# Eight late tiles of a Hyena convolution: their three-tap convolutions and gates go from VectorE to GpSimd

## The reference, cut to what matters

```python
def short_conv(u, w, b):
    L = u.shape[1]
    pad = HY_SHORT // 2
    up = jnp.pad(u, ((0, 0), (pad, pad), (0, 0)))
    return sum(up[:, j:j + L] * w[j] for j in range(HY_SHORT)) + b
...
    p = h @ w_in
    u = short_conv(p[..., :(HY_ORDER + 1) * HY_WIDTH], conv_w, conv_b)
    gate = p[..., (HY_ORDER + 1) * HY_WIDTH:]
    parts = jnp.split(u, HY_ORDER + 1, axis=-1)
    k_f = hyena_filters(L, f_w1, f_b1, f_w2, f_b2, f_w3, f_b3, freq)
    z = parts[0]
    for o in range(HY_ORDER):
        z = parts[o + 1] * long_conv(z, k_f[:, o], skip[o])
    return (z * jax.nn.silu(gate)) @ w_out
```

## Time and profile before

| what | us |
|---|---|
| median of 3 runs | 4747.56 (4747.15 to 4749.07) |
| the profiled execution | 4751.5 |
| its span on the core | 4749.7 |
| PE busy in the span | 4617.1 (97%) |
| DVE busy in the span | 2067.6 (44%) |
| ACT busy in the span | 1006.4 (21%) |
| POOL busy in the span | 3.9 (0%) |

### The profile page before, as it was taken

The page is one execution under the profiler, slowest core; times in us unless marked ns, Lnnn a source line. Parts: engine busy times, 40 slices in busy tenths (PEclk is TensorE's granted clock), DMA queues, the critical chain, the costliest instruction groups (busy, mean ns, idle before and its releaser), DMA issues.

```text
span 4749.7 us, 39586 instructions
## 1 busy us (share of the span) xinstructions
PE 4617.1 (97%) x16572; PEld 2291.0 (48%) x16572; DVE 2067.6 (44%) x2485; ACT 1006.4 (21%) x1349; POOL 3.9 (0%) x7
## 2 busy tenths in 40 slices
PE   7999999999999999989999999999999999999998
PEld 3456666443434444544555555444444444444444
DVE  3555555134333266663344444513643363333412
ACT  3145555111111100001333322322310010000000
POOL 0000000000000000000000000000000000000000
PEclk9999999998999999999999999999999999999999
DMA  6200000221322522221111011112231131111211
GB/s 250 73 27 10 10 6 10 106 75 60 111 73 93 200 107 102 102 99 58 45 40 37 32 36 40 40 45 76 78 104 40 41 123 36 45 45 45 78 44 56
DMA packets 106814, 320.29 MB, mean 67 GB/s; under 512 B 26086, under 2 KB 44262, under 8 KB 99083
## 3 DMA queue, kind: packets, MB, share of 16 engines
q1 hardware_dynamic: 89708, 306.22, 18.2%
q10 hardware_dynamic: 16928, 11.54, 0.8%
HBM read 257.36 MB, written 60.36 MB: 67 GB/s over the span
## 4 chain that ended last, share of the span: by engine, by line
PE 69%; DVE 6%; DMA 1%; issue 1%; ACT 0%; DVEq 0%; SPq 0%
PE late_dense L122 32%; PE late_four L3328 10%; PE late_two L3328 5%; PE late_four L3558 3%; PE late_four L1431 3%; PE late_four L1620 2%; PE late_four L2378 2%; PE late_dense L3558 1%; PE late_two L1708 1%; PE late_two L1700 1%; PE late_four L1448 1%; PE late_four L1443 1%; PE late_two L3558 1%; PE late_two L1637 1%; PE late_two L2732 0%
## 5 line engine op out<-in xcount | busy, mean ns | idle before, releaser
L122 PE MATMUL late_dense<-arena 128*128 128x512 f32 x4008 | 1767.8, 598 | 3.5 <-DVE arena L3149 1.3
L122 PEld LDWEIGHTS late_dense<-arena 128*128 128x128 f32 x4008 | 760.3, 192 | 936.7 <-issue 927.9
L3328 PE MATMUL late_four<-arena 128*128 128x512 f32 x1160 | 504.5, 592 | 0.0
L135 ACT ACTIVATE arena<-late_dense 128x512 f32<-128x512 f32 x198 | 118.0, 597 | 1130.8 <-PE late_dense L122 1102.9
L3328 PEld LDWEIGHTS late_four<-arena 128*128 128x128 f32 x1160 | 220.4, 190 | 277.4 <-issue 273.8
L122 PE MATMUL attn_dense<-arena 128*128 128x512 f32 x640 | 281.3, 597 | 4.2 <-ACT arena L637 2.1
L3328 PE MATMUL late_two<-arena 128*128 128x512 f32 x576 | 253.4, 592 | 0.0
L3377 DVE TENSOR_TENSOR arena<-late_four,arena 128x512 f32<-128x512 f32 x145 | 98.7, 690 | 298.9 <-PE late_four L3328 294.4
L839 PE MATMUL attn_dense<-matrices,arena 128*128 128x128 f32 x1280 | 187.6, 283 | 18.2 <-ACT arena L885 16.1
L122 PEld LDWEIGHTS attn_dense<-arena 128*128 128x128 f32 x640 | 121.0, 191 | 158.6 <-issue 153.5
L1431 PE MATMUL late_four<-arena 128*128 128x512 f32 x384 | 173.3, 605 | 8.1 <-DMA arena<-in_hy_tables 4.5
(11 more groups left out here) (389 smaller groups left out, 4733.9 us busy)
## 6 DMA issues: line engine op xcount, KB each, us to landing
arena<-in_ada_w SPq DMA_DIRECT2D x12, 2048.0 KB, 8.0
arena<-in_w_ffn_in SPq DMA_DIRECT2D x44, 512.0 KB, 4.0
arena<-in_hy_tables SPq DMA_DIRECT2D x16, 1280.0 KB, 6.0
arena<-in_hy_w_in SPq DMA_DIRECT2D x32, 512.0 KB, 3.2
spectrum<-arena SPq DMA_DIRECT2D x8, 2048.0 KB, 8.1
arena<-spectrum SPq DMA_DIRECT2D x8, 2048.0 KB, 12.7
arena<-in_w_gates SPq DMA_DIRECT2D x32, 512.0 KB, 3.3
spill<-arena SPq DMA_DIRECT2D x26, 512.0 KB, 4.4
```

The lines of the kernel that those rows point to most:

```text
L122: mm = pe.matmul(self.ps[:, n % SEG], self.wbuf[:, slot, k], job.rhs[:, k, cols], start=(job.first and k == 0), stop=(job.last and k == kt ...
L135: act.activation(job.out[:, cols], self.ps[:, n % SEG], job.func, scale=job.scale, bias=job.bias).then_inc(self.emptied[n % SEG], 1)
L3328: mm = pe.matmul(product_bank(M, name, i), left[:, k], right[:, k], start=(k == 0), stop=(k == 3))
```

## The change

Tiles 0 to 15 are convolved as before: `conv` and `gate` move out of `hyena_dve` and take the engine as an argument. For tiles 16 to 23, the calls in the rounds of `hyena_dve` go away, and a new list `hyena_pool` does them on GpSimd, ahead of `mixer_pool`, tile after tile: the convolution, then the gate. `late_conv` has five operations in place of three: the scaled and shifted middle tap as before, then for each outer tap a product into a scratch row (`Y.turned[:, 0]`) and a sum. `hyena_pool` first waits until the row is free, that is until the last transposed tile has been stored (`turned_out`).

```diff
@@ -1771,6 +1771,62 @@
         evict(act, 3)
 
 
+def conv(eng, Y, m):
+
+    name, out, tap = f"c{m}", Y.u[:, m % 2], Y.taps[:, m]
+    raw = Y.ring_row(name)
+    Y.dense.done(eng, name)
+    eng.wait_ge(Y.taps_in, 32)
+    eng.wait_ge(Y.taps_scaled, m // 4 + 1)
+    if m >= 2:
+        eng.wait_ge(Y.aux_filled, Y.use["t", m - 2] + 1)
+    eng.tensor_scalar(out, raw, tap[:, 1:2], tap[:, 3:4], ALU.mult, ALU.add).then_inc(Y.conv_step, 1)
+    eng.wait_ge(Y.conv_step, 2 * m + 1)
+    eng.scalar_tensor_tensor(out[:, 1:L], raw[:, 0:L - 1], tap[:, 0:1], out[:, 1:L], ALU.mult, ALU.add).then_inc(Y.conv_step, 1)
+    eng.wait_ge(Y.conv_step, 2 * m + 2)
+    ins = eng.scalar_tensor_tensor(out[:, 0:L - 1], raw[:, 1:L], tap[:, 2:3], out[:, 0:L - 1], ALU.mult, ALU.add)
+    ins.then_inc(Y.convolved, 1)
+
+
+def gate(eng, Y, m):
+
+    name = f"g{m}"
+    Y.dense.done(eng, name)
+    eng.wait_ge(Y.convolved, 16 + m + 1)
+    u = Y.u[:, m % 2]
+    eng.tensor_tensor(u, u, Y.ring_row(name), ALU.mult).then_inc(Y.gated, 1)
+
+
+def hyena_pool(pool, Y):
+
+    for s in range(2):
+        pool.wait_ge(Y.turned_out[s], 16 * 8)
+    for m in range(DT):
+        late_conv(pool, Y, m)
+        gate(pool, Y, m)
+
+
+def late_conv(pool, Y, m):
+
+    n, base, tmp = 16 + m, 32 + 4 * m, Y.turned[:, 0]
+    out, tap, raw = Y.u[:, m % 2], Y.taps[:, n], Y.ring_row(f"c{n}")
+    Y.dense.done(pool, f"c{n}")
+    pool.wait_ge(Y.taps_in, 32)
+    pool.wait_ge(Y.convolved, 16 + m)
+    if m < 2:
+        pool.wait_ge(Y.aux_filled, Y.use["t", n - 2] + 1)
+    else:
+        pool.wait_ge(Y.last_out[m % 2], 16 * (m // 2))
+    pool.tensor_scalar(out, raw, tap[:, 1:2], tap[:, 3:4], ALU.mult, ALU.add).then_inc(Y.conv_step, 1)
+    pool.tensor_scalar(tmp[:, 0:L - 1], raw[:, 0:L - 1], tap[:, 0:1], None, ALU.mult).then_inc(Y.conv_step, 1)
+    pool.wait_ge(Y.conv_step, base + 2)
+    pool.tensor_tensor(out[:, 1:L], out[:, 1:L], tmp[:, 0:L - 1], ALU.add).then_inc(Y.conv_step, 1)
+    pool.wait_ge(Y.conv_step, base + 3)
+    pool.tensor_scalar(tmp[:, 0:L - 1], raw[:, 1:L], tap[:, 2:3], None, ALU.mult).then_inc(Y.conv_step, 1)
+    pool.wait_ge(Y.conv_step, base + 4)
+    pool.tensor_tensor(out[:, 0:L - 1], out[:, 0:L - 1], tmp[:, 0:L - 1], ALU.add).then_inc(Y.convolved, 1)
+
+
 def hyena_dve(dve, Y):
     dense, group, aux, S, X = Y.dense, Y.group, Y.aux, Y.S, Y.X
     def mix():
@@ -1778,32 +1834,6 @@
         dve.wait_ge(Y.taps_filled, 16)
         for way, op in enumerate((ALU.add, ALU.subtract)):
             dve.tensor_tensor(Y.mix[:, way], Y.w3[:, 0], Y.w3[:, 1], op).then_inc(Y.mixed, 1)
-
-    def conv(m):
-        name, out, tap = f"c{m}", Y.u[:, m % 2], Y.taps[:, m]
-        raw = Y.ring_row(name)
-        dense.done(dve, name)
-        dve.wait_ge(Y.taps_in, 32)
-        if m < 16:
-            dve.wait_ge(Y.taps_scaled, m // 4 + 1)
-        if 2 <= m < 18:
-            dve.wait_ge(Y.aux_filled, Y.use["t", m - 2] + 1)
-        elif m >= 18:
-            dve.wait_ge(Y.last_out[m % 2], 16 * ((m - 16) // 2))
-        dve.tensor_scalar(out, raw, tap[:, 1:2], tap[:, 3:4], ALU.mult, ALU.add).then_inc(Y.conv_step, 1)
-        dve.wait_ge(Y.conv_step, 2 * m + 1)
-        dve.scalar_tensor_tensor(out[:, 1:L], raw[:, 0:L - 1], tap[:, 0:1], out[:, 1:L], ALU.mult,
-                                 ALU.add).then_inc(Y.conv_step, 1)
-        dve.wait_ge(Y.conv_step, 2 * m + 2)
-        ins = dve.scalar_tensor_tensor(out[:, 0:L - 1], raw[:, 1:L], tap[:, 2:3], out[:, 0:L - 1], ALU.mult, ALU.add)
-        ins.then_inc(Y.convolved, 1)
-
-    def gate(m):
-        name = f"g{m}"
-        dense.done(dve, name)
-        dve.wait_ge(Y.convolved, 16 + m + 1)
-        u = Y.u[:, m % 2]
-        dve.tensor_tensor(u, u, Y.ring_row(name), ALU.mult).then_inc(Y.gated, 1)
 
     def largest(it, q):
 
@@ -1836,11 +1866,11 @@
                     dve.scalar_tensor_tensor(Y.later[:, m], Y.later[:, m], Y.one_plus[:, 1, 0, m:m + 1], Y.later_mean, ALU.mult,
                                              ALU.mult).then_inc(Y.scaled, 1)
             if it and q == 4:
-                conv(4 * it - 2)
+                conv(dve, Y, 4 * it - 2)
         largest(it, LT - 2)
         largest(it, LT - 1)
         if it:
-            conv(4 * it - 1)
+            conv(dve, Y, 4 * it - 1)
         dve.wait_ge(Y.aux_read, Y.use["total", it] + 1)
         dve.wait_ge(Y.skip_in, 16 * (it + 1))
         dve.tensor_tensor(Y.skip, Y.skip, Y.total, ALU.mult).then_inc(Y.scale_step, 1)
@@ -1859,22 +1889,20 @@
             s = 2 * it + f
             group_dve(dve, Y, s, 0)
             if f:
-                conv(4 * it + 1)
+                conv(dve, Y, 4 * it + 1)
             if s:
                 dve.wait_ge(Y.x_stored, 16 * s)
             dve.wait_ge(Y.group_filled, 2 * s + 2)
             dve.wait_ge(Y.group_read, s + 1)
             spectrum_dve(dve, Y, group[:, 0:2], group[:, 3:1:-1])
             if not f:
-                conv(4 * it)
-    conv(14)
-    conv(15)
+                conv(dve, Y, 4 * it)
+    conv(dve, Y, 14)
+    conv(dve, Y, 15)
     for j, (o, half) in enumerate(ROUNDS):
         for f in range(2):
             n, m, g = 2 * STEPS + 2 * j + f, 2 * j + f, 2 * STEPS + 4 * j + 2 * f
             group_dve(dve, Y, g, 0)
-            if f:
-                gate(m - 1)
             group_dve(dve, Y, g + 1, 1)
             if n == 2 * STEPS:
                 dve.wait_ge(Y.x_stored, 16 * 2 * STEPS)
@@ -1882,12 +1910,7 @@
             spectrum_dve(dve, Y, S[:, 4:6], S[:, 7:5:-1])
             base = 12 * (2 * j + f)
             products_dve(dve, Y, n, f, j, base)
-            if not f:
-                conv(16 + m)
             fold_dve(dve, Y, f, base)
-            if f:
-                conv(16 + m)
-        gate(2 * j + 1)
         evict_dve(dve, Y, j, o, half)
     gate_out, Z = Y.mod[:, 5 * DT:6 * DT, 0], Y.shared
     norm = Z.norm
@@ -3741,6 +3764,7 @@
 
             @block.gpsimd
             def _(pool):
+                hyena_pool(pool, Y)
                 mixer_pool(pool, Y, M)
 
             @block.tensor
```

## The result

| | before | after |
|---|---|---|
| median, us | 4748.3 (4747.2 to 4750.6, 4 runs) | 4814.6 (4810.3 to 4815.9, 4 runs) |
| ratio | | 1.0137, 95% interval 1.012 to 1.0155 |
| span of the profiled execution, us | 4749.7 | 4812.6 |

The changed kernel is 66 us slower by the medians and 62.9 us by the spans of the two profiled executions. The prediction was 4822, in a range of 4757 to 4860.

What follows compares the result with a forecast made beforehand. VectorE's list was taken to bound each round at two TensorE waits. Per round, 6.7 us at the first, 1.8 of lower clock and 10.1 at the second make 18.6; four are 74.4, from 4747.6 to 4822 us, range 4757 to 4860.

Steps and rivals of the forecast that it cites:

- What bounds the rounds: In the four rounds, VectorE is level with TensorE at one place and late at a second, despite idling half the time.
- both places: TensorE's waits for VectorE each round: before the transform at 1811.63 (0.98 to 0.1 us), before the inverse (3.32 or 10.19).
- What is taken from VectorE: Half 0's convolution, 3.4 us per round, relieves the first place; TensorE can use 1.5 us in all; half 1 gives nothing.
- taking turns at full price: VectorE's two-arena-operand operations wait while GpSimd reads, 1 us per us: 18.6 us per round, 4822 us; 60%.
- The rival in which nothing is shared: In VectorE's two-operand stretches, GpSimd costs nothing or always yields; TensorE regains 1.5 us, 4746 us; 20%, within 0.2%.
- the one in which GpSimd gets in only at three places per half: In the long stretch, GpSimd enters only where VectorE waits for its own result: 5 us per half, 4774 us; 18%.
- P: GpSimd's time per tile, three one-input operations at 1.35 us and three two-input at 2.0: 10.1 us, bounds 5.4 and 13.5.
- the prediction's own sign: In the profile after, GpSimd lengths outside 0.9 to 1.8 (one-input) or 0.9 to 2.7 us (two-input) mean P failed.
- The clock's part: A new wait at the first place lowers the granted clock afterwards, some matmuls at 1.2 GHz: 1.8 us per round.
- GpSimd's own length costs nothing: In the rounds, an 8.1 us convolution fits before ScalarE needs its row: 28.8 us of room, 21 in round 0.
- The waits foreseen: TensorE's waits after the change: 7 to 8 us on L1465; on L1968 13 in rounds 0 to 2, 20 in round 3.

Runs made afterwards that it cites:

- The table of parts: Parts of the change alone on GpSimd, rest on VectorE: even convolutions 4771.9 us, odd convolutions 4776.6, both 4801.0, gates 4758.3; the whole change 4814.6.

## Why the prediction was right, point by point

**What bounds the rounds** was right: both places took the loss, and no other wait of TensorE in the rounds grew. The table of parts shows them to be independent. One reading slipped: behind the transform at 1811.63 come the last three pieces of the round (48 matmuls), not six; nothing in the sum uses it.

**What is taken from VectorE** was right: of its 3.4 us in half 0 the full amount counted (the even convolutions' 6.6 us of reads added 3.3 us of wait in round 1), and nothing in half 1 did.

**The direction and the mechanism** were right, taking turns at full price. The rival in which nothing is shared is excluded by VectorE's lengths, and so is the one in which GpSimd gets in only at three places per half where VectorE waits for its own result: three of the six longer operations (L1969, L1971 and L1985) stand at none of these places. The rival's observation had something in it: operations with factors per partition pass over some of VectorE's operations. It changes where the price is paid, not how much.

**The mis-sized term is P.** I took 10.1 us per tile and it is 8.8 (8.76 at the fold). A one-input operation costs 0.72 to 0.88, not 1.35, below even the low end of 0.9 from the memset; a two-input one costs 2.1, for which 2.0 was taken. And the reasoning behind P was wrong in kind: I took GpSimd's length as the price, one us for one us. GpSimd by itself needs 13.9 us per tile, above my upper bound of 13.5, and VectorE pays 8.8. By the prediction's own sign, a length outside the bounds (2.85 us for L1821 alone, with 1.8 as the bound), P is the step that failed. That the time still came within 7 us of the forecast is partly luck: the two errors have opposite signs. With the true length and one us for one us, the same sum gives 4 x (10.5 + 1.8 + 13.9) = 105 us, 4852. That the length doesn't matter is shown by the operations shortened by 1.7 us.

**The clock's part**: 1.8 us taken, 2.0 measured in round 1 and 1.8 to 2.7 in the others. It is no fixed price: with the even convolutions alone on GpSimd, the same wait of 3.3 us for the fold was followed by an inverse of 27.70 us in round 1 and of 30.91 in round 2. By terms, a round is 5.2 + 2.0 + 8.8 = 16.0 us where I had 6.7 + 1.8 + 10.1 = 18.6.

**GpSimd's own length costs nothing** held, with less room than I said. A convolution took 20.7 us in round 1 and 22.0 in round 0, where I had 8.1; the room was 28.8 and 21. In round 0 it ended at 1694.8, and the eviction of c17, at 1693.49 before, came at 1694.81. TensorE's next transform waited for VectorE until 1698.18 anyway.

**The waits foreseen** were 7 to 8, 13 and 20 us; they are 4.4 to 6.9, 12.1 and 18.9.

## What to carry to other kernels

Before moving elementwise work to an idle GpSimd, look at what VectorE does at that time: beside operations with two SBUF inputs, GpSimd's reads are taken out of VectorE's time (8.8 us per tile here), and the move pays only if VectorE was relieved of more on the critical path. Here 3.4 us of relief per round stood against 17.5 of reads. In the inverse, where VectorE reads PSUM, the odd tiles' work was free, and useless. An engine that is idle for half of the program can still be what the others wait for: an order that takes its work out of the two places where it is waited for gained what a second engine could not.

## What the runs showed of the hardware that I had not expected

- The price of a GpSimd operation for VectorE is not its length: about 0.84 us for a one-input operation on 1024 columns that takes 1.19 or 2.85 us by itself, 2.1 us for a two-input one of 2.34 that writes over one of its inputs, 1.69 if both inputs are the same row and the output another, and 0 for a memset.
- VectorE's one-input step of 0.81 us paid too: 2.38 us beside a two-input operation of GpSimd.
- On GpSimd, a product with a factor per partition took 2.85 us with one operation where VectorE was out of its way. In the rounds it took 6.7 us, and 5.0 with a second operation that changes nothing. Whether the 1.19 us of the other two-operation form is also reached with 1023 columns and nobody in the way wasn't run.
- Beside the same work of VectorE, GpSimd's one-input operations with factors per partition took 4.5 us each and those with constants 2.6, and the price for VectorE is the same. Why the former pass over some of VectorE's operations stays open.
